# Weight chunks of two dense projections: sum and scale two chunks ahead, split one ahead, totals taken out by ACT, gating weights loaded a stage earlier

## The reference

```
def first_block(x, ...):
    x = layer_norm(x, ln_in_g, ln_in_b)
    h = einsum('bsd,de->bse', x, w_in)
    au, av, ag, ba, bb, bg, cq, ck, cv, cg = split(h)
    ya = spatial_gating(au, av, ag, ..., w_spatial, b_spatial)
    yb = conformer_conv(ba, bb, bg, conv_w, ...)          # 31 taps
    yc = window_attention(cq, ck, cv, cg, sink, rel_bias) # window 128
    return layer_norm(ALPHA * x + concat(ya, yb, yc) @ w_out, ...)

def second_block(x, ...):
    q, k, v, g_attn, c_h, c_b, c_c, g_conv = split(rmsnorm(x, g) @ w_in)
    q, k = rope(q), rope(k)
    o = softmax-weighted sum of dilated_window_attn(q, k, v, w, d)
        for (w, d) in ((128, 1), (512, 4), (2048, 16))
    conv_out = c_b * causal_conv(c_c * c_h) * silu(g_conv)
    return x + rmsnorm(concat(o * silu(g_attn), conv_out) @ w_out, g_post)
```

## Time and profile before

| | us |
|---|---|
| median of three runs (lowest, highest) | 2424.43 (2419.78, 2424.54) |
| the profiled execution | 2428.2 |
| its span | 2426.4 |
| PE busy | 2106.3 (87%) |
| DVE busy | 1433.8 (59%) |
| ACT busy | 902.4 (37%) |
| POOL busy | 864.1 (36%) |

### The profile page before, as it was taken

The page is one execution under the profiler, slowest core; times in us unless marked ns, Lnnn a source line. Parts: engine busy times, 40 slices in busy tenths (PEclk is TensorE's granted clock), DMA queues, the critical chain, the costliest instruction groups (busy, mean ns, idle before and its releaser), DMA issues.

```text
span 2426.4 us, 43240 instructions
## 1 busy us (share of the span) xinstructions
PE 2106.3 (87%) x16228; PEld 1550.3 (64%) x16228; DVE 1433.8 (59%) x3539; ACT 902.4 (37%) x1933; POOL 864.1 (36%) x956
## 2 busy tenths in 40 slices
PE   5999999785896999499999999999697878776898
PEld 3545758675785888488444444748576666665776
DVE  7514858764896544762567743121398888893421
ACT  3322222221785000332233331212297877772111
POOL 3311121262423987331112121111127666962222
PEclk9999999897898999799999999999898998897999
DMA  5441321136642232432343421211467776564443
GB/s 170 138 102 60 109 70 45 44 116 177 165 110 101 87 109 97 152 109 66 121 138 114 130 81 44 79 44 53 98 158 170 176 165 158 136 182 152 139 141 111
DMA packets 285631, 279.95 MB, mean 115 GB/s; under 512 B 39936, under 2 KB 237952, under 8 KB 285168
## 3 DMA queue, kind: packets, MB, share of 16 engines
q1 hardware_dynamic: 279200, 270.01, 38.7%
q0 software_dynamic: 1680, 5.51, 0.6%
q10 hardware_dynamic: 4544, 1.66, 0.4%
HBM read 171.22 MB, written 93.31 MB: 109 GB/s over the span
## 4 chain that ended last, share of the span: by engine, by line
PE 24%; DVE 11%; POOL 8%; issue 3%; DMA 3%; ACT 2%; SPq 2%; DVEq 0%; ACTq 0%; POOLq 0%
PE bank L172 23%; DVE s2m L2261 4%; DVE p2l L2267 3%; POOL cm L2139 1%; POOL qs L2307 1%; POOL gt L2147 1%; DMA qr<-qf 1%; DVE qf L1752 1%; POOL kept L2143 1%; POOL kept L2141 1%; SPq L1781 1%; DVE qr L1750 1%; POOL kept L2139 1%; ACT s2sh L1732 1%; POOL yo L2492 1%
## 5 line engine op out<-in xcount | busy, mean ns | idle before, releaser
L2204 PE MATMUL bank<-ident,p2r 128*128 128x128 f32 x900 | 171.9, 306 | 88.7 <-DVE p2l L2267 84.5
L172 PE MATMUL bank<-xh,w2h 128*128 128x512 f16 x640 | 245.6, 384 | 0.0
L172 PE MATMUL bank<-xl,w2h 128*128 128x512 f16 x640 | 245.3, 383 | 0.0
L172 PE MATMUL bank<-xh,w2l 128*128 128x512 f16 x640 | 245.2, 383 | 0.0
L172 PE MATMUL bank<-w1h,xh 128*128 128x256 f16 x768 | 213.0, 277 | 11.3 <-DVE s1st L902 11.3
L172 PE MATMUL bank<-w1l,xh 128*128 128x256 f16 x768 | 213.0, 277 | 0.0
L172 PE MATMUL bank<-w2h,xh 128*128 128x256 f16 x768 | 211.2, 275 | 2.0 <-issue 2.0
L172 PE MATMUL bank<-w1h,xl 128*128 128x256 f16 x768 | 212.8, 277 | 0.0
L172 PE MATMUL bank<-w2l,xh 128*128 128x256 f16 x768 | 211.1, 275 | 0.0
L172 PE MATMUL bank<-w2h,xl 128*128 128x256 f16 x768 | 211.0, 275 | 0.0
L2267 DVE SCALAR_TENSOR_TENSOR p2l<-bank,p2h 128x512 f16<-128x512 f32 (+1 forms) x288 | 164.2, 570 | 49.2 <-ACT p2h L2233 48.9
(11 more groups left out here) (339 smaller groups left out, 5635.4 us busy)
## 6 DMA issues: line engine op xcount, KB each, us to landing
scr_part<-ob SPq DMA_DIRECT2D x48, 264.0 KB, 2.7
cm<-scr_part SPq DMA_DIRECT2D x48, 264.0 KB, 5.0
w2r<-in_w_in SPq DMA_DIRECT2D x12, 1024.0 KB, 6.3
qr<-qf SPq DMA_DIRECT2D x192, 64.0 KB, 2.0
v<-scr_v SPq DMA_DIRECT2D x176, 65.0 KB, 2.2
ax<-in_x SPq DMA_DIRECT2D x16, 512.0 KB, 4.2
xr<-in_x SPq DMA_DIRECT2D x16, 512.0 KB, 4.6
bx<-scr_x SPq DMA_DIRECT2D x16, 512.0 KB, 6.4
```

The lines of the kernel that those rows point to most:

```text
L172: ins = nc.tensor.matmul(dst, x, y, start=k == 0 and m == 0, stop=k == n - 1 and m == 2)
L2204: ins = nc.tensor.transpose(bank[:, w * hh + 128 * c:w * hh + 128 * c + 128], p[:, hh, 128 * c:128 * c + 128], ident[:])
```

## The change

Per chunk: sum, total and scale are made two chunks ahead of use, and the split, which stood in the same chunk as these, one ahead and at the start. The total is taken out of PSUM by ACT with a copy, and the lower limit of 1e-30 that DVE applied becomes a sixth operation of POOL. In conv and spatial one function, `prepare`, writes the steps: split of c+1 with the first group, sum of c+2 with the second, its total and the load of c+3 with the third, its scale with the fourth. In rope and gate the sum goes to tile 2, PE's total behind tile 3, ACT's total to tile 5, its scaling to tile 6, the load to tile 4; in rope the bound moves from tile 5 to tile 4, and the first one from behind tile 0 to behind tile 1. In norm the first group of chunk 0 is cut in two steps around the total and split of chunk 1; chunk 4 is summed, totalled and scaled there, and chunk 5 loaded at the very end. w_spatial (256 KB) is loaded at conv's head and no longer at spatial's.

```diff
 class Weights:
-        def dve_total(self, n, bank):
-            dve.wait_ge(*self.added[n])
-            nc.vector.tensor_scalar(self.size[:, n, 1:2], bank[:, 0:1], 1e-30, None, ALU.max).then_inc(*self.d_t.up())
+        def act_total(self, n, bank):
+            act.wait_ge(*self.added[n])
+            nc.scalar.activation(self.size[:, n, 1:2], bank[:, 0:1], ACT.Copy).then_inc(*self.a_t.up())
 
         def pool_scale(self, n):
             pool.wait_ge(*self.total[n])
+            nc.gpsimd.tensor_scalar(total, total, 1e-30, None, ALU.max).then_inc(*self.g_u.up())
+            pool.wait_ge(*self.g_u.now())
...
 norm_stage, work:
             if g == 0:
-                work += [("load", 1), ("total", 1)]
+                work.append(("load", 1))
             if g < 3:
                 work.append(("scale", g + 1))
-            if g == 0:
-                work.append(("split", 1))
...
-            work.append(("group", 0, g))
+            if g > 0:
+                work.append(("group", 0, g))
+            else:
+                work += [("group", 0, 0, 0), ("total", 1), ("split", 1), ("group", 0, 0, 1)]
             if g == 1:
-                work += [("load", 2), ("total", 2)]
-        work += [("split", 2), ("group", 1, 3)]
+                work.append(("load", 2))
+            if g == 2:
+                work.append(("total", 2))
+        work += [("split", 2), ("load", 3), ("group", 1, 3)]
...
-        work += [("consts",), ("load", 3), ("total", 3)]
-        work += [("group", 2, 0), ("scaled", 3)] + [("group", 2, g) for g in range(1, 4)]
+        work += [("consts",), ("total", 3), ("group", 2, 0), ("scaled", 3), ("halve", 3), ("group", 2, 1)]
+        work += [("load", 4), ("group", 2, 2), ("total", 4), ("group", 2, 3), ("scaled", 4)]
 norm_stage, act_program, item "turn":
-                        if m == 3:
+                        if m == 1:
+                            wts.act_total(0, total_bank[0][0])
+                        if m == 5:
                             wts.act_hi(0)
 norm_stage, sp_program ("load" is the sum's item; SP's loads stand here):
+                elif item == ("scaled", 4):
+                    wts.sp_load(5)
...
+    def prepare(wts, c, g):
+        items = [("halve", c + 1), ("sum", c + 2), ("total", c + 2), ("scaled", c + 2)][g:g + 1] + [("load", c + 3)] * (g == 2)
+        return [x for x in items if x[1] < len(wts.chunks)]
 conv_stage, work:
-            work.append(("load", first + n + 1))
             for g in range(4):
-                if g == 1:
-                    work.append(("total", first + n + 1))
-                if g == 2:
-                    work.append(("scaled", first + n + 1))
+                work += prepare(wts, first + n, g)
 conv_stage, sp_program:
+            nc.sync.dma_start(ws[:], A["w_spatial"][0].rearrange("h i j -> i h j")).then_inc(*sem("ws_in").up(16))
 spatial_stage, sp_program:
-            nc.sync.dma_start(ws[:], A["w_spatial"][0].rearrange("h i j -> i h j")).then_inc(*w_ld.up(16))
...
 rope_stage, pe_program (gate's total likewise):
-                if m == 0:
+                if m == 1:
                     pe_bound(0)
-                if m % 8 == 1:
-                    wts.pe_total(first + x["n"] + 1, *total_bank[x["n"]])
+                if m % 8 == 3:
+                    wts.pe_total(first + x["n"] + 2, *total_bank[x["n"]])
 rope_stage, act_program (gate's likewise):
-                if m % 8 == 0:
-                    wts.act_sum(first + m // 8 + 1)
-                if m % 8 == 4:
-                    wts.act_scale(first + m // 8 + 1)
+                if m % 8 == 2:
+                    wts.act_sum(first + m // 8 + 2)
+                if m % 8 == 5:
+                    wts.act_total(first + m // 8 + 2, total_bank[m // 8][0])
+                if m % 8 == 6:
+                    wts.act_scale(first + m // 8 + 2)
 rope_stage, dve_program:
-                if m % 8 == 2:
-                    wts.dve_total(first + x["n"] + 1, total_bank[x["n"]][0])
-                if m % 8 == 5 and x["n"] < 5:
+                if m % 8 == 4 and x["n"] < 5:
                     dve_bound(x["n"] + 1)
 rope_stage, pool_program (gate's likewise):
             for n in range(6):
-                wts.pool_scale(first + n + 1)
                 wts.pool_split(first + n + 1)
+                wts.pool_scale(first + n + 2)
 rope_stage, sp_program (gate's likewise):
-                if m % 8 == 0:
-                    wts.sp_load(first + m // 8 + 2)
+                if m % 8 == 4:
+                    wts.sp_load(first + m // 8 + 3)
```

More of the change, by code:

```diff
@@ L194, in __init__ @@
             self.added = [(self.p_t, self.p_t.n + n + 1) for n in range(len(chunks))]
-            self.total = [(self.d_t, self.d_t.n + n + 1) for n in range(len(chunks))]
-            self.scaled = [(self.g_u, self.g_u.n + 5 * n + 5) for n in range(len(chunks))]
+            self.total = [(self.a_t, self.a_t.n + n + 1) for n in range(len(chunks))]
+            self.scaled = [(self.g_u, self.g_u.n + 6 * n + 6) for n in range(len(chunks))]
             self.landed, self.by_act, self.half, self.ready = [], [], [], []
@@ L487, in pe_program @@
                 elif item[0] == "group":
-                    _, n, g = item
+                    _, n, g = item[:3]
                     pe.wait_ge(*wts.ready[n])
                     pe.wait_ge(*d_xl.at(8 * g + 8))
-                    for kind, step, _, _, (bank, before) in steps[n, g]:
+                    for kind, step, _, _, (bank, before) in steps[item]:
                         if step == 1 and g == 0 and n in valued:
@@ L511, in act_program @@
                     wts.act_sum(item[1])
+                elif item[0] == "total":
+                    wts.act_total(item[1], total_bank[item[1]][0])
                 elif item[0] == "split":
@@ L608, in dve_program @@
             for item in work:
-                if item[0] == "total":
-                    wts.dve_total(item[1], total_bank[item[1]][0])
-                elif item[0] == "split":
+                if item[0] == "split":
                     wts.dve_lo(item[1])
@@ L630, in dve_program @@
                 elif item[0] == "group":
-                    _, n, g = item
-                    if n in valued and g == 0:
+                    _, n, g = item[:3]
+                    if n in valued and g == 0 and item[3:] in ((), (1 if turned else 0,)):
                         dve_fit(n)
-                    for kind, step, mm, e, (bank, _) in steps[n, g]:
+                    for kind, step, mm, e, (bank, _) in steps[item]:
                         if kind == "f":
@@ L686, in sp_program @@
             for item in work:
-                if item[0] == "load" and item[1] > 1:
-                    wts.sp_load(item[1] + 1)
+                if item == ("load", 2):
+                    wts.sp_load(3)
+                elif item == ("scaled", 4):
+                    wts.sp_load(5)
                 elif item[0] == "scale":
@@ L823, in act_program @@
             for at, item in enumerate(work):
-                if item[0] == "load":
+                if item[0] == "sum":
                     wts.act_sum(item[1])
+                elif item[0] == "total":
+                    wts.act_total(item[1], plan[at][0])
                 elif item[0] == "scaled":
@@ L876, in dve_program @@
             for at, item in enumerate(work):
-                if item[0] == "total":
-                    wts.dve_total(item[1], plan[at][0])
-                elif item[0] == "conv":
+                if item[0] == "conv":
                     _, c, i = item
@@ L999, in spatial_stage @@
         for n in range(2):
-            if n == 0:
-                work.append(("load", first + 1))
             for g in range(4):
-                if n == 0 and g == 1:
-                    work.append(("total", first + 1))
-                if n == 0 and g == 2:
-                    work.append(("scaled", first + 1))
+                work += prepare(wts, first + n, g)
                 for step in range(2):
@@ L1818, in gate_stage @@
                     tiles.append(x)
-                    if len(tiles) % 8 == 2 and first + n + 1 < len(wts.chunks):
-                        total_bank[n] = bk.take(wts.total[first + n + 1])
+                    if len(tiles) % 8 == 4 and first + n + 2 < len(wts.chunks):
+                        total_bank[n] = bk.take(wts.total[first + n + 2])
             wts.spent[first + n] = p_mm.at(len(tiles))
@@ L1856, in dve_program @@
                 bank, what, k, c = x["bank"][0], x["what"], x["k"], x["c"]
-                if m % 8 == 2 and x["n"] in total_bank:
-                    wts.dve_total(first + x["n"] + 1, total_bank[x["n"]][0])
                 s = 512 * (x["i"] % 4)
```

90 lines of the change are left out of this document (45 added, 45 removed).

## The result

The changed kernel takes 2427.72 us (median of 11 runs, 2422.30 to 2430.63); the kernel before, run beside it, 2420.64 us (11 runs, 2410.58 to 2425.34). The profiled execution has a span of 2427.4 us against 2426.4.

A forecast was written before the change was run, and what follows sets the result against it. PE, busy 87% of the span, was taken to bound the kernel. The terms summed to 33.5 us off the profiled 2428.2, giving 2394.7, less 3.8 for the median: 2391 us. Its own range was 2377 to 2408, the stated one 2374 to 2412.

The forecast's parts named there:

- (a): At the chunk totals: PE's five large waits for ACT's sum go, covered by two tiles (10.4 us); +16.9 us.
- (b): In rope: PE's two later waits for the bound go, if DVE keeps up; +3.1 us.
- rival 4: In rope: the evacuation becomes PE's limit and the kernel gets slower, 2431 us; chance 0.04.
- (c): Behind the five totals and rope's last bound: PE's half-clock stretches run at full clock; +11 us.
- (h): New PE waits at gate's start (1 us) and in norm b's second turn (0.3 us); -1.3 us.
- (f): Norm b's start: chunk 1's later total and split hold PE's last transposed tile; -3.2 us (from -5 to +1.5).
- (d): Spatial's start: PE's wait for ws goes and its clock rises; +6.8 us.
- (e): Norm a's start: same reorder as in norm b, sign left open; +0.9 us (from -1.5 to +3).
- (i): Conv: DVE loses a small total per chunk and meets fewer POOL subtracts; +0.5 us (from -2 to +3).
- (g): Rope's start: chunk 5 lands late and POOL's split blocks DVE's small multiply; -1.2 us (from -3 to +2).

## Why the prediction was wrong

The step that failed is the cover in (a) and the condition in (b): "Two tiles are 10.4 us of cover", "nothing else is late at them", and "3.1 us go, if DVE keeps up". DVE did not keep up, and the cover was used up, because of a term that stood at nothing: SP's wait at the moved load. The prediction names SP's load only at rope's start. It wrote in rival 4 that "the load at tile 4" might meet the same tiles, but gave it no wait of its own and priced only POOL's lock. What it left out: `sp_load` waits not only for the split of the chunk whose buffer it takes, which is all that the description of the kernel names, but in rope also for that chunk's bound (`read[n - 2]`). Before, that bound was made a chunk earlier; the change puts load and bound at the same tile, so SP waits, and on SP the read-back of tile 4 is queued behind. DVE stands 6.9 to 8.1 us behind each bound, over the stage 62.2 us for qr, against 34.2 with the load at tile 6. The ratio differs by 1.3%, some 30 us, of the 41 that the forecast missed by (1.003 against 0.986).

With this wait away, the terms for rope and gate come out: 5.75 of (a), 3.1 of (b) and half of the 3.40 and 5.89 us of PE's work at 0.50 behind rope's last bound and gate's total (c), less 1 of (h), are 12.5 us, and the three kernels without the wait gain 12.5 to 13.5 there (568.5 to 556.0, 555.9 and 555.0). Of the other 10 us missed, 4.1 lie ahead of conv's end and 1.0 in (f), as below; the rest is not accounted for, and the window attention alone differs by more between traces of the same code (last section).

By the prediction's own terms:

- (a) Right for the five totals that it names: the four in norm a and norm b and the one at gate's start (5.75 before) wait no longer. Wrong for five others, in rope, that had not waited before. It also takes the two largest waits (7.1 and 6.6) for chunk 0's totals and leaves them standing. They are chunk 1's, which stood ahead of chunk 0's first tile (29.62 and 31.80 us in norm a); the change puts them behind it, and PE waits for chunk 0's split in their place, so they give nothing all the same.
- (b) In the changed kernel the bounds of rope wait once, 2.6 us, at the start. The row came as forecast, but it is worth nothing there, since the time went to the totals in front of them.
- (c) Right where the waits went: 1.00 at 72.2, 471.5 and 1438. Wrong in sum: "the forecast falls if stretches at 0.50 appear in number where none were", and four stand in rope, one in spatial.
- (d) 6.8 predicted; the lead grows from 6.0 us at conv's end (456.16 to 450.19) to 13.9 at the window's start, 7.9. PE's waits for my fell from 11.5 to 8.1 and did not take it back. The stretch from conv's end to the window's start takes 135.8 to 136.9 us in the nine kernels with the change and 144.3 to 144.9 in the three without it, so this term is clear of the spread. It is not the load of w_spatial alone that gives it, as its experiment shows.
- (a), (c), (e) and (i) up to conv's end: 2.67 + 2.72 + 3.3 + 0.9 + 0.5 = 10.1 predicted, 6.0 measured. Norm a's cut seems to cost rather than give: with norm a whole conv ends at 449.23 us in the trace, and in the eight with the cut between 450.19 and 452.68. The ratio moved by more, from 0.9873 to 0.9837 (9 us), of which these traces show 1.0 to 3.4; the two kernels were not run side by side. The rest of the 4.1 us stays open and lies within that spread.
- (f) -3.2 predicted, -4.2 measured, at the place and with the gap of about 7 us that was named (7.02).
- (g) Right in mechanism: DVE and POOL start together and DVE's small multiply, 0.17 us before, takes 3.76 beside POOL's subtract.

```profile
1151.21 2.29 DVE L1707 TENSOR_REDUCE qwm<-w2r 128x8 f32<-128x2048 f32 x1 [6.98 <-DMA w2r<-in_w_in]
1153.53 3.76 DVE L1709 TENSOR_TENSOR qwm<-qwm,most 128x8 f32<-128x8 f32 x1
...
1151.24 1.89 POOL L275 CAST w2h<-w2r 128x2048 f16<-128x2048 f32 x1 [16.15 <-DMA w2r<-in_w_in]
1153.21 4.06 POOL L277 TENSOR_TENSOR w2l<-w2r,w2h 128x2048 f16<-128x2048 f32 x1
```

  The wait is 2.65 us (3.72 before), and not 5.4, because the reduce began 3.7 us before PE's tile 1 ended (1157.54 - 2.65 = 1154.9), where the sum had 1.3. So the term is a gain of 1.1 where -1.2 stood.
- (h) No wait at gate's start, where 1 was taken. In norm b PE waits 1.65 us at 1144.38 for DVE's bvo, and in norm a 1.3 and 0.6 around 49 us, where 0.3 stood.
- Rival 4 (chance 0.04) was the right one in kind: rope's evacuation became PE's limit. Its 2431 us lie near the 2427.72 measured, but that is luck, since neither its cause (meetings of DVE with POOL) nor its price is what happened. It asked for 6.65 us per tile before the gain is gone; a chunk took 46.9 to 50.4 us, about 6.0 a tile, and the whole gain and more went. It held that PE would be free until 36 us of lag were used up in the banks. But PE stops for a total or a bound long before its banks are full: the total behind tile 3 needs ACT's sum at tile 2, so PE is held within two tiles of ACT. The lead that counts is that of the nearest wait.
- Against rival 4 stood "the same operations run in each chunk before, at 5.36". That is true of the operations and says nothing of the waits between them on SP.

## What to carry to other kernels

When an instruction moves, list the waits inside it and ask of each when its condition becomes true at the new place, and then what stands behind it on its engine. A load that waits for its buffer costs nothing where the buffer is free, and a stall for everything else on the issuing queue where it isn't. Either the reader of the buffer goes ahead of the load (the bound at tile 2) or the load behind the reader (tile 6); both gave 1.3%. And where two waits end within a microsecond of each other, removing one may show nothing, as with w_spatial here.

## What the runs showed of the hardware

- DVE's 128x8 multiply of two SBUF tensors, at most 167 ns in six places before, took 3.76 us beside POOL's subtract of 128x2048 (4.06 us), and ended with it.
- A 1 MB load per chunk issued at tile 6 by SP or by ACT, beside the read-backs of 64 KB, gave the same time (ratios 0.9904 and 0.9905).
- Executions of one kernel can lie 0.9% apart (2417.78 to 2438.63 for the one with norm b whole). Part of it arises in the window attention and output projection, whose code is the same in all: from 372.9 to 386.8 us in the twelve traces. It took 375.6 us in the trace of the kernel before (600.72 to 976.32) and 386.8 in that of the kernel with norm b whole (587.22 to 973.99).
